# Two norm stages of a hybrid RWKV/PEER layer with their head sums in 16 PSUM rows, and the sigmoid and offset moved into the scan

## What is computed

```python
kk = (k * k_k).reshape(b, t, H_A, 64)
kk = kk / maximum(norm(kk, axis=-1), 1e-12)                 # key norm
...                                                          # scan -> y_fwd + y_bwd
mu  = mean(y, -1);  var = mean(square(y - mu), -1)          # group norm over a head's 64
yn  = (y - mu) * rsqrt(var + GN_EPS) * ln_x_w + ln_x_b
y_a = (yn + bonus) * sigmoid(g)
u   = gelu(zb[..., :1024])
vg  = layernorm(gelu(zb[..., 1024:]), ln_v_w, ln_v_b)       # over all 1024 channels
sp  = einsum('hpq,bnqhc->bnphc', w_s, vg in chunks of 128) + b_s
y_g = u * sp
o   = concat([y_a, y_g]) @ w_out                            # "gated half" is y_g
```

## Time and profile before

| what | value |
|---|---|
| median of 3 runs | 3400.42 us |
| span of the profiled execution | 3393.9 us |
| PE busy, of the span | 2967.0 us, 87% |
| DVE / ACT / POOL busy | 71% / 41% / 24% |
| gating stage, from the first PE matmul to the scan's first work | 732.5 to 809.4 us |
| scan | 809.4 to 1293.4 us |
| output stage until its first product | 1293.9 to 1348.0 us |

### The profile page before, as it was taken

How to read it: one execution, slowest core, us unless ns; L and a number is a source line. 1 busy time by engine, 2 the same in 40 slices (tenths; PEclk the granted TensorE clock), 3 DMA queues, 4 the chain that set the end, 5 groups by cost and what they waited for, 6 DMA issues and landing times.

```text
span 3393.9 us, 60012 instructions
## 1 busy us (share of the span) xinstructions
PE 2967.0 (87%) x23592; PEld 2591.9 (76%) x23592; DVE 2423.7 (71%) x3113; ACT 1396.9 (41%) x1827; POOL 797.8 (24%) x548
## 2 busy tenths in 40 slices
PE   6987998985888884969997777799999899999997
PEld 2335998973777773958997677799999688787876
DVE  5995554228667666355998677677777799898987
ACT  6885333332333334334334455433333333333333
POOL 0000000001222222004664222211112234444442
PEclk9998999996999997989998889899999899999998
DMA  9993332310000001323446899899999999999996
GB/s 376 420 421 120 124 129 105 124 62 4 6 8 6 9 4 51 118 88 137 157 145 231 300 310 310 284 385 386 388 387 386 415 417 417 417 417 417 417 417 250
DMA packets 207446, 811.72 MB, mean 239 GB/s; under 512 B 81472, under 2 KB 101056, under 8 KB 118336
## 3 DMA queue, kind: packets, MB, share of 16 engines
q1 hardware_dynamic: 170432, 541.14, 42.3%
q0 software_dynamic: 36864, 268.45, 19.7%
HBM read 769.16 MB, written 40.37 MB: 239 GB/s over the span
## 4 chain that ended last, share of the span: by engine, by line
PE 21%; DMA 17%; DVE 9%; issue 4%; ACT 2%; POOL 1%; SPq 0%; DVEq 0%; ACTq 0%
DMA work<-act_table 10%; PE ps L1583 5%; PE ps L1584 5%; PE ps L1585 5%; DMA x<-u_rows,idx 3%; DMA raw<-expert_u 3%; DVE work L2156 2%; DVE x L2079 2%; DVE wlo L2161 1%; PE ps L1840 1%; PE ps L1841 1%; PE ps L1842 1%; DVE wlo L1572 1%; POOL wlo L1572 1%; PE ps L1933 1%
## 5 line engine op out<-in xcount | busy, mean ns | idle before, releaser
L1583 PE MATMUL ps<-hhi,whi 128*128 128x256 f32 x2048 | 590.8, 288 | 48.9 <-DVE wlo L1572 28.7
L1584 PE MATMUL ps<-hlo,whi 128*128 128x256 f32 x2048 | 585.8, 286 | 0.0
L1585 PE MATMUL ps<-hhi,wlo 128*128 128x256 f32 x2048 | 585.4, 286 | 0.0
L1583 PEld LDWEIGHTS ps<-hhi,whi 128*128 128x128 f32 x2048 | 400.1, 195 | 52.9 <-DVE wlo L1572 30.0
L1933 PE MATMUL ps<-whi,hhi 128*128 128x512 f32 x1024 | 402.3, 393 | 35.8 <-DVE wlo L2161 19.6
L282 PE MATMUL ps<-hhi,whi 128*128 128x384 f32 x1056 | 358.3, 339 | 77.9 <-DVE hlo L1440 42.8
L1966 POOL DMA_INDIRECT work<-expert_v,idx x128 | 310.0, 2422 | 418.4 <-DVE work L2156 404.0
L1934 PE MATMUL ps<-wlo,hhi 128*128 128x512 f32 x1024 | 399.9, 391 | 0.0
L1584 PEld LDWEIGHTS ps<-hlo,whi 128*128 128x128 f32 x2048 | 399.8, 195 | 0.0
L1935 PE MATMUL ps<-whi,hlo 128*128 128x512 f32 x1024 | 399.6, 390 | 0.0
L1585 PEld LDWEIGHTS ps<-hhi,wlo 128*128 128x128 f32 x2048 | 399.4, 195 | 0.0
(11 more groups left out here) (299 smaller groups left out, 5950.0 us busy)
## 6 DMA issues: line engine op xcount, KB each, us to landing
raw<-expert_u SPq DMA_DIRECT2D x128, 1024.0 KB, 5.0
z<-w_ada SPq DMA_DIRECT2D x72, 1024.0 KB, 15.1
raw<-expert_v SPq DMA_DIRECT2D x64, 1024.0 KB
work<-expert_v SPq DMA_DIRECT2D x64, 1024.0 KB
raw<-w_in SPq DMA_DIRECT2D x50, 1024.0 KB, 4.7
raw<-w_ada SPq DMA_DIRECT2D x24, 1024.0 KB, 13.7
raw<-w_out SPq DMA_DIRECT2D x16, 1024.0 KB, 4.7
raw<-w_query SPq DMA_DIRECT2D x16, 1024.0 KB, 5.0
```

The lines of the kernel that those rows point to most:

```text
L1583: pe.matmul(bank, whi[:, r, k, :], moving_hi, start=(k == 0), stop=False)
L1584: pe.matmul(bank, whi[:, r, k, :], moving_lo, start=False, stop=False)
L1585: last = pe.matmul(bank, wlo[:, r, k, :], moving_hi, start=False, stop=(k == KD - 1))
```

## The change

- `heads16`, a new constant table, has in its columns 16j to 16j+15 a mask that puts the two heads of pair j into rows 2j and 2j+1. Eight matmuls accumulate all sums of squares into one 16-row PSUM tile. Root, clip and reciprocal are made once on 16x384; PE spreads them back to 128 partitions with 8 matmuls against `spread` (16 x 1024, a new input, loaded in both stages).
- In the gating stage the loops are written out; subtraction and squares go in 4 pieces; the scale and offset of `vn` move from DVE to ACT; `b_s` comes in by a one-row matmul into the same PSUM tile, and the gate is one multiplication. The tanh comes first; the sigmoid of `Z_G` is gone from here.
- In the scan ACT makes the sigmoid of the current pair's `Z_G` once per pair, and POOL adds `ln_x_b` to the bonus in `Z_K`.
- In the output stage one scaled multiply-add replaces scale, offset and the bonus add; POOL keeps one multiplication. The first product takes the gated half first (k = 8 to 15, then 0 to 7) and waits per block.

```diff
 # gating stage, PE
-                with pe.Fori(0, PAIRS // 2) as it:
...
-                        pe.matmul(ps[:, 6 + u, 0:T], table("head_sum"), norm[:, bass.ds(it * 2 + u, 1), :].rearrange("p o t -> p (o t)"),
-                                  start=True, stop=True).then_inc(kk_sum.sem, 1)
+                for j in range(PAIRS):
+                    pe.wait_ge(kk_sq.sem, j + 1)
+                    last = pe.matmul(ps[0:16, 6, 0:T], table("heads16")[:, 16 * j:16 * j + 16], norm[:, j, :],
+                                     start=(j == 0), stop=(j == PAIRS - 1))
...
+                def over_heads(j):
+                    if j == 0:
+                        pe.wait_ge(kk_inv.sem, 1)
+                    if j >= RING:
+                        pe.wait_ge(kk_done.sem, j - RING + 1)
+                    pe.matmul(ps[:, 6 + j % RING, 0:T], spread[:, j * P:(j + 1) * P], inv[:, :], start=True, stop=True
+                              ).then_inc(kk_spread.sem, 1)
+
+                def mix(j):
...
+                    for c in range(TILES):
+                        out = ps[:, 4 + u, c * P:(c + 1) * P]
+                        pe.matmul(out, table("ones")[0:1, :], bsp[:, j, :], start=True, stop=False)
+                        last = pe.matmul(out, vt[:, u, c * P:(c + 1) * P], wsp[:, j, :], start=False, stop=True)
+                    last.then_inc(mixed.sem, 1)
+
+                for j in range(HB):
+                    over_heads(j)
+                    turn(j)
+                    if j:
+                        mix(j - 1)
+                mix(HB - 1)
 # gating stage, DVE
-                    ch.link(nc.vector.tensor_scalar(over[:, :, :], nm, 1e-12, None, ALU.max))
-                    ch.link(nc.vector.reciprocal(over[:, :, :], over[:, :, :]))
-                    ch.link(nc.vector.tensor_tensor(kn, kn, over[:, :, :], ALU.mult))
...
+                ch.link(nc.vector.tensor_scalar(inv[:, :], inv[:, :], 1e-12, None, ALU.max))
+                nc.vector.reciprocal(inv[:, :], inv[:, :]).then_inc(kk_inv.sem, 1)
...
+                for j in range(HB):
+                    if j + 2 < HB:
+                        scale(j + 2)
+                    if j + 1 < HB:
+                        key(j + 1)
+                    gate(j)
 # scan
+                    nc.gpsimd.tensor_scalar(zb(Z_K, it), zb(Z_K, it), colr("ln_x_b", it), None, ALU.add)
...
                             if n == 0:
                                 front_gates(it + 1, 1)
+                                nc.scalar.activation(zb(Z_G, it), zb(Z_G, it), ACT.Sigmoid)
...
+                    if not more:
+                        nc.scalar.activation(zb(Z_G, it), zb(Z_G, it), ACT.Sigmoid)
 # output stage, PE
+                for j in range(PAIRS):
+                    if j == 0:
+                        pe.wait_ge(gn_inv.sem, 1)
+                    if j >= 4:
+                        pe.wait_ge(gn_done.sem, j - 3)
+                    pe.matmul(ps[:, 4 + j % 4, 0:T], spread[:, j * P:(j + 1) * P], inv[:, :], start=True, stop=True
+                              ).then_inc(gn_spread.sem, 1)
+                hi, lo = st.parts[0]
+                pe.wait_ge(*st.split(0, 0))
+                for i in range(KD):
+                    k = (i + PAIRS) % KD
+                    pe.wait_ge(y_split.sem, 1 if k >= PAIRS else k + 2)
...
 # output stage, DVE
-                    nc.vector.reciprocal(dev_, dev_).then_inc(gn_done.sem, 1)
...
+                scale(0)
+                for j in range(PAIRS):
+                    if j + 1 < PAIRS:
+                        scale(j + 1)
+                    add(j)
+                    if j < RING:
+                        st.low(dve, 0, j)
+                    if j >= 3:
+                        low(j - 3)
+                for j in range(PAIRS - 3, PAIRS):
+                    low(j)
```

More of the change, by code:

```diff
@@ L648, in _ @@
+                last.then_inc(kk_sum.sem, 1)
                 for j in range(HB):
+                    pe.wait_ge(act_to_pe.sem, act_to_pe.v + j // 2 + 1)
                     last = pe.matmul(ps[:, 1, 0:T], table("mean_db"), wide[:, j, :], start=(j == 0), stop=(j == HB - 1))
                 last.then_inc(pe_to_act.sem, 1)
[L651 to L665, removed]
-                        last.then_inc(mixed.sem, 1)
@@ L675, in _ @@
[L675 to L681 removed]
+                nc.scalar.activation(z[:, Z_LW, :], z[:, Z_LW, :], ACT.Tanh)
@@ new lines, in _ @@
+                for j in range(PAIRS):
+                    nc.scalar.activation(norm[:, j, :], z[:, Z_K + j, :], ACT.Square, scale=col("k_k", j)).then_inc(kk_sq.sem, 1)
+                for c in range(HB // 2):
+                    act.wait_ge(dve_to_act.sem, dve_to_act.v + c + 1)
+                    nc.scalar.activation(wide[:, 2 * c:2 * c + 2, :], vz[:, 2 * c:2 * c + 2, :], ACT.Square).then_inc(act_to_pe.sem, 1)
+                act.wait_ge(kk_sum.sem, 1)
+                nc.scalar.activation(inv[:, :], ps[0:16, 6, 0:T], ACT.Sqrt).then_inc(kk_root.sem, 1)
@@ L693, in _, with copy @@
+                def copy(j):
+                    act.wait_ge(vn_turned.sem, j + 1)
+                    if j >= RING:
+                        act.wait_ge(mixed.sem, j - RING + 1)
+                    nc.scalar.activation(vt[:, j % RING, :], ps[:, 2 + j % RING, 0:T], ACT.Copy).then_inc(vt_ready.sem, 1)
+                affine(0)
+                for j in range(HB):
+                    if j + 1 < HB:
+                        affine(j + 1)
+                    copy(j)
             @block.vector
@@ L702, in _ @@
                 dve.wait_ge(pe_to_dve.sem, pe_to_dve.v + 1)
[L703 to L704 removed]
+                for c in range(HB // 2):
+                    v2 = vz[:, 2 * c:2 * c + 2, :]
+                    nc.vector.tensor_tensor(v2, v2, ps[:, 0:1, 0:T].to_broadcast([P, 2, T]), ALU.subtract).then_inc(dve_to_act.sem, 1)
+                dve.wait_ge(kk_root.sem, 1)
@@ new lines, in gate @@
+                def gate(j):
+                    dve.wait_ge(mixed.sem, j + 1)
+                    nc.vector.tensor_tensor(z[:, Z_U + j, :], z[:, Z_U + j, :], ps[:, 4 + j % RING, 0:T], ALU.mult).then_inc(gated.sem, 1)
+                scale(0)
+                scale(1)
+                key(0)
+                for j in range(HB):
+                    if j + 2 < HB:
+                        scale(j + 2)
+                    if j + 1 < HB:
+                        key(j + 1)
+                    gate(j)
@@ L1362, in _ @@
             def _(sp):
+                sp.dma_start(spread[:, :], spread_in).then_inc(loads.sem, 16)
                 st.load(sp, KD, w_out)
@@ L1401, in _ @@
                     st.high(act, 0, n)
-                with act.Fori(0, PAIRS) as it:
-                    act.wait_ge(y_ready.sem, it + 1)
-                    nc.scalar.activation(hhi[:, bass.ds(it, 1), :], z[:, bass.ds(it, 1), :], ACT.Copy).then_inc(y_high.sem, 1)
+                for j in range(PAIRS):
+                    act.wait_ge(y_ready.sem, j + 1)
+                    nc.scalar.activation(hhi[:, j, :], z[:, j, :], ACT.Copy).then_inc(y_high.sem, 1)
                 act.wait_ge(y_split.sem, PAIRS + 1)
```

199 lines of the change are left out of this document (85 added, 114 removed).

## The result

The changed kernel takes 3378.11 us (median of 4, 3365.98 to 3382.55), the kernel before beside it 3415.91 us (median of 4, 3399.02 to 3436.62). The ratio is 0.9884, with an interval of 0.9838 to 0.993: faster by 1.2%. A second set of runs of the same changed kernel gave 0.9931 (0.9888 to 0.9974). The prediction was 3344.0 us with a range of 3334 to 3364, so the measured time lies 34 us above the forecast and 14 us above the range. The direction was right, the size was not: of the forecast gain of 57 us the medians show 37.8. The stages that the change touches show 32.6; the loop of the gating stage alone fell 30 us short of its forecast.

The account below looks back on a forecast made before the run. It took the gating stage and the output stage's start as chains of engines waiting for each other. -14.5 - 18.9 + 1.3 + 2 - 27 = -57 us brought span 3393.9 to 3337, plus 6.5 gave 3344; range 3334 to 3364.

Parts of the forecast that it names:

- Gating stage to the first turn: Gating stage before its loop: first turn at 753.0 instead of 767.5, a gain of 14.5 us.
- The loop: Gating stage after the first turn: PE becomes the bound, 22.8 us instead of 41.7, a gain of 18.9 us.
- That is 0.67 + 0.33 + 1.3 = 2.3 us: Gating loop: PE's time per block for spread (2 records), turn (3 records) and product with bias (12 records).
- before it fell to half clock after such a gap and stayed there for 4 us of full work: 2 us more: Gating loop: PE's 4 us pause ahead of it brings half clock for 4 us of work, costing 2 us.
- The first rival: Gating loop: PE stays at half clock, giving back 14 us, total 3358; chance 0.17.
- about 5: Gating loop: gain left with half clock throughout, 17.6 us more instead of 2, if slower matmuls hide most waits.
- Scan: Scan: table load ahead of the first sigmoid costs 1.3 us, sigmoids delaying copies in seven pairs cost 2 us.
- the lower bound that the prediction gave, 0: Scan: low end for the per-pair sigmoids' cost, taken as 2 us with ends 0 and 3.2.
- The slow rival: Scan: POOL's new add takes more than 12.4 us a pair, delaying the next; at 26 us total 3439; chance 0.03.
- Output stage: Output stage: first product starts at 1321.0, second ends at 1340.6 instead of 1367.8, a gain of 27 us.
- The order's share of the gain: Output stage: taking the gated half first is worth only some 3 us of the 27 us gain.
- The second rival: Output stage: POOL and DVE block each other, first product ends at 1338.3 instead of 1332, total 3350; chance 0.13.

Follow-up runs that it names:

- e_bias64: Changed kernel with gating-loop bias products over 64 rows (bias in row 0, zeros in the others) instead of one; 55.5 us first turn to scan, median 3376.93 us.
- e_eq64: e_bias64 with the group mixing product cut to the same 64 rows, so not computing the layer; 43.3 us first turn to scan, 3374.62 us (one run).
- e_all128: Changed kernel with gating-loop bias products and spreads all over 128 rows (spread rows 16 to 127 zeros); 22.7 us first turn to scan, median 3346.0 us.
- e_best: e_all128 plus five idle PE products ahead of the gating loop and 128-row spreads in the output stage; 21.0 us first turn to scan, median 3357.16 us.
- e_warm: Changed kernel plus five idle 128-row products on PE just ahead of the first turn; 52.5 us first turn to scan, median 3371.53 us.
- e_order: Changed kernel with the output products' blocks back in order 0 to 15; 43.5 us to the first product instead of 38.0, median 3395.43 us.
- e_base: The kernel before, unedited, profiled again; mixer's stretch 827.2 us instead of 806.9, median 3413.59 us.
- e_bias_dve: Changed kernel without the bias product, DVE adding the bias as before, 16-row spreads kept; 32.5 us first turn to scan, median 3374.14 us.
- e_bias128: Changed kernel with gating-loop bias products over 128 rows instead of one, same number of records; 28.3 us first turn to scan, median 3352.49 us.

## Why the prediction was wrong

**Gating stage to the first turn: right.** Forecast 14.5 us, measured 14.4 (35.0 to 20.6).

**The loop: the step that failed.** It forecast 18.9 us of gain and there were 11.1 of loss, a miss of 30.0. That PE would be the bound was right. The term "That is 0.67 + 0.33 + 1.3 = 2.3 us" was mis-sized for the change as it is: it took 0.11 us for a record of 128 columns from the earlier trace rows and 0.33 for one of 384, both from matmuls over 128 rows at clock 1.00, and put them on matmuls over 1 and 16 rows. A block took 6.75 us. Two costs make it up. The switch between row counts inside the pairs: 55.5 - 43.3 = 12.2 us, from e_bias64 to e_eq64. The clock, with what the 16-row spreads still add: 43.3 - 22.7 = 20.6 us, from e_eq64 to e_all128. Their sum is 32.8, and 22.7 is 2.8 below the forecast's 25.5: for a loop whose matmuls all have 128 rows the term holds (2.31 us a block in e_all128). The next step, "before it fell to half clock after such a gap and stayed there for 4 us of full work: 2 us more", priced the pause about right (1.7 us from e_all128 to e_best). What failed in it is that the clock would come back after those 4 us: it stayed at 0.50 through the whole loop, and in e_warm, with no such gap, it fell from 1.00. The first rival had the clock (at a chance of 0.17), priced at 14 us against at most 20.6, and nothing for the switch; its bound of "about 5" of gain for half clock throughout was wrong by 16 us, 12.2 of them the switch.

**Scan: nothing instead of +3.3 us.** The table load does stand ahead of the first sigmoid, but in time in which PE waits for a transfer:

```profile
808.76 1.28 ACT L923 ACT_TABLE_LOAD   x1 [9.10 <-PEq L613]
...
810.76 1.64 PE L1124 MATMUL ps<-z,lora 64*128 64x384 f32 x2 [2.95 <-DMA lora<-w2a]
```

The forecast had not looked at what PE waits for there. The sigmoids per pair cost nothing that shows: the scan took 480.3 us against 482.1 and 479.9 in the two profiles of before, and 479.0 to 482.7 in all others. Here the lower bound that the prediction gave, 0, was the right value. The slow rival was POOL's new operation, bounded by rows at 0.5 and 1.0 us; it takes 1.24 (8 in 9.9, L914), above both rows, and is covered too, far from its limit of 12.4.

**Output stage: right, in size and mostly in mechanism.** Forecast 27 us, measured 27.5. The timeline of after has the steps:

```profile
1305.06 3.36 DVE L1462 TENSOR_TENSOR hlo<-z,hhi 128x3072 fp32r<-128x3072 f32 x1
...
1309.96 2.97 POOL L1425 TENSOR_TENSOR z<-z 128x384 f32<-128x384 f32 x1 [30.51 <-DVE z L1471]
...
1312.46 0.88 DVE L1471 SCALAR_TENSOR_TENSOR z<-z,cols 128x384 f32<-128x384 f32 x1
...
1313.42 2.98 POOL L1425 TENSOR_TENSOR z<-z 128x384 f32<-128x384 f32 x1 [0.49 <-DVE z L1471]
...
1316.06 1.64 PE L1403 MATMUL ps<-inv,spread 16*128 16x384 f32 x2 [1.83 <-DVE z L1467]
...
1318.38 1.26 POOL L1425 TENSOR_TENSOR z<-z 128x384 f32<-128x384 f32 x1 [0.49 <-DVE z L1471]
```

The last spread starts at 1316.06 and the first product right behind it at 1317.64, 26.5 us after the stage began, where the forecast had 27. The order's share of the gain was mis-sized, 5.5 us and not 3 (e_order). The second rival is seen and is cheap. POOL's first two multiplications take 2.97 and 2.98 us beside DVE's weight lows, one 0.99 and five 1.26; DVE's multiply-adds take 0.61 once and 0.88 to 1.37 then, where the forecast had 0.5 to 0.6. The rule of the Trainium skill, SBUF: State Buffer, section "SBUF: two separate sides", that a DVE operation with two SBUF inputs and a GpSimd operation that reads SBUF take turns on a shared port pair, agrees with that, and the rows add that both engines pay. PE still worked on its first 24 records, at half clock until about 1323, and waited for a low part only once, 0.23 us at 1327.13, so what they paid lay beside it. No kernel was run with the bonus left out of POOL, so this reading rests on the rows alone.

**The base of the sum: 15.5 us too low.** The forecast stood on the median of three runs of before, 3400.42 us; beside the change the kernel before took 3415.91. Of the 34 us between forecast and result some 15 are this base, and some 19 the gain that did not come. With the later base the forecast would be some 3359 us, and the loop's 30 us wrong all the same. The profiled execution that the sum was made against was a short one in one stretch too: its mixer stretch lasted 806.9 us, 20 less than in e_base, so the 820.3 in the changed kernel are not shown to be a cost of the change. Without that stretch the stages give 1081.4 - 1048.8 = 32.6 us of gain, or 29.3 against e_base. The medians say somewhat more, 3415.91 - 3378.11 = 37.8 in the first comparison and 36 in the second, with intervals that hold both.

## What to carry to other kernels

Price a matmul by a measured record with its own number of contraction rows, and where there is none, give the loop it stands in a half-clock case with the distance of a pair of unlike row counts in it. In a loop that PE bounds, bringing a 1-row or 16-row operand to the 128 rows of its neighbours costs no record. Here the bias was filled into all 128 rows and averaged, and the spread padded with rows of zeros, and both together took 55.5 us to 22.7. Before a sum is made against one profile, compare its stretch of heavy transfers (a DMA share of 0.97 to 1.01 here) with other executions: it may be a lucky one.

## What the runs showed of the hardware

- PE busy 5.00 of 5.00 us in window after window at a granted clock of 0.50, to the end of loops that took 32.5 to 55.5 us to the scan's first matmul (after, e_bias64, e_eq64, e_bias_dve), and a fall from 1.00 to 0.50 under unbroken work (e_warm). The same loop with 128 rows in each matmul ran at 1.00 (e_best; e_all128 behind its first few us); with 128 rows in all but the spreads it rose after ten us (e_bias128).
- Two fp32 records of 128 columns, where the row count changes with each product: 0.72 us from start to start at half clock and 0.41 at full, against 0.43 and 0.22 where it stays the same. The weight loads of two records take 0.50 us with 1 row as with 128 (after, at half clock).
- POOL takes 1.24 us for a scale-or-offset of 128x384 (`TENSOR_SCALAR`), more than the 0.99 of its multiplication of two such tiles.
